# Second attention's query projections: where the modulation sums, the split of the queries and the weight units stand on VectorE and ScalarE

## The reference, cut to what matters

```
sh1, sc1, g1, sh2, sc2, g2 = split(silu(c) @ w_mod[1] + b_mod[1], 6)
h   = modulate(rmsnorm(x, b_norm_g), sh1, sc1)
cq  = rmsnorm(h @ w_dq, q_g)          # 1024 -> 768
q   = (cq @ w_uq)                     # 768  -> 16 heads of 64 + 32
...                                   # rope on the 32, attention, @ w_o
x   = x + g1 * mix
```

## Time and profile before

| | |
|---|---|
| median of 3 runs | 2210.35 us (2209.51 to 2211.14) |
| the profiled execution, its own time | 2212.91 us |
| span of its profile, first to last instruction | 2211.1 us |
| TensorE busy (matmul) | 1876.4 us, 85% of the span |
| VectorE busy | 1505.4 us, 68% |
| ScalarE busy | 848.0 us, 38% |
| GpSimd busy | 561.1 us, 25% |
| mean granted TensorE clock | 0.918 of full speed |
| DMA | 616.18 MB, mean 279 GB/s |
| chain of waits that ended last | TensorE 57%, VectorE 17%, GpSimd 7%, issue 7%, DMA 4%, ScalarE 2% |

### The profile page before, as it was taken

One profiled execution on the slowest core, in us unless ns is written; L12 is line 12 of the kernel. 1 busy time (PEld: TensorE's weight loads), 2 busy tenths in 40 slices (PEclk: granted clock), 3 DMA queues, 4 the chain that ended last, 5 costly groups with the idle time before them and its releaser, 6 DMA issues.

```text
span 2211.1 us, 22537 instructions
## 1 busy us (share of the span) xinstructions
PE 1876.4 (85%) x7847; PEld 1245.6 (56%) x7847; DVE 1505.4 (68%) x2494; ACT 848.0 (38%) x1294; POOL 561.1 (25%) x613
## 2 busy tenths in 40 slices
PE   4998999999978899999996998885786778686786
PEld 1866788888755577888885544682232223232232
DVE  3347778999863775679998995586665565655544
ACT  1354444788634634557783014341221121111120
POOL 0000100000000003030000000036666667666664
PEclk8999999999989999999998999997888888797898
DMA  9761688999855339679994324359999999999997
GB/s 329 273 232 39 239 292 309 392 382 370 321 181 198 127 111 214 206 241 385 379 390 149 118 95 134 124 197 370 360 377 375 377 349 371 360 389 357 369 378 290
DMA packets 193760, 616.18 MB, mean 279 GB/s; under 512 B 19096, under 2 KB 21568, under 8 KB 193008
## 3 DMA queue, kind: packets, MB, share of 16 engines
q1 hardware_dynamic: 114336, 325.98, 40.9%
q0 software_dynamic: 78608, 285.90, 34.8%
q10 hardware_dynamic: 704, 2.86, 0.4%
HBM read 609.43 MB, written 5.25 MB: 278 GB/s over the span
## 4 chain that ended last, share of the span: by engine, by line
PE 57%; DVE 17%; POOL 7%; issue 7%; another core or an unknown queue 6%; DMA 4%; ACT 2%; SPq 0%; DVEq 0%; POOLq 0%; ACTq 0%
PE PS L998 20%; PE PS L1028 10%; DVE peer_rows L2332 6%; PE PS L781 6%; PE PS L802 4%; PE PS L772 4%; POOL peer_rows L713 4%; POOL peer_rows L727 2%; PE PS L1255 2%; DMA peer_rows<-in_peer_u,MOD 1%; DMA ring<-in_w_mod 1%; PE PS L1160 1%; POOL AR L727 1%; PE PS L825 1%
## 5 line engine op out<-in xcount | busy, mean ns | idle before, releaser
L2332 DVE SCALAR_TENSOR_TENSOR peer_rows<-peer_rows,PS 128x1024 f32<-128x1024 f32 x256 | 309.9, 1212 | 80.3 <-DMA peer_rows<-in_peer_u,MOD 73.1
L1974 DVE TENSOR_TENSOR weights_low<-ring,weights_high 128x1024 fp32r<-128x1024 f32 x231 | 280.1, 1229 | 62.2 <-ACT weights_high L1372 59.8
L1372 ACT ACTIVATE weights_high<-ring 128x1024 fp32r<-128x1024 f32 x231 | 242.8, 1061 | 108.8 <-PE PS L998 72.4
L713 POOL DMA_INDIRECT peer_rows<-in_peer_u,MOD x256 | 247.5, 967 | 118.6 <-issue 72.6
L1255 PE MATMUL PS<-peer_rows,HT 128*128 128x512 f32 x368 | 194.5, 663 | 77.0 <-issue 44.1
L1974 DVE TENSOR_TENSOR weights_low_more<-ring,weights_high_more 128x1024 fp32r<-128x1024 f32 x153 | 185.4, 1223 | 36.9 <-ACT weights_high_more L1372 35.4
L1776 DVE TENSOR_TENSOR weights_low<-ring,weights_high 128x1024 fp32r<-128x1024 f32 (+1 forms) x81 | 95.8, 1197 | 139.9 <-ACT weights_high L1279 139.5
L1581 ACT ACTIVATE MOD<-MOD 128x16 f32<-128x16 f32 x16 | 3.4, 215 | 488.7 <-DVE peer_rows L2332 421.6
L1372 ACT ACTIVATE weights_high_more<-ring 128x1024 fp32r<-128x1024 f32 x153 | 161.0, 1060 | 72.8 <-PE PS L998 46.5
L1255 PEld LDWEIGHTS PS<-peer_rows,HT 128*128 128x128 f32 x368 | 74.4, 210 | 193.6 <-issue 184.5
L1255 PE MATMUL PS<-AR,HT 128*128 128x512 f32 x216 | 117.6, 680 | 56.0 <-issue 54.2
(11 more groups left out here) (402 smaller groups left out, 3953.6 us busy)
## 6 DMA issues: line engine op xcount, KB each, us to landing
ring<-in_exp_w_gate SPq DMA_DIRECT2D x128, 512.0 KB, 5.9
ring<-in_exp_w_up SPq DMA_DIRECT2D x128, 512.0 KB, 5.9
ring<-in_exp_w_down SPq DMA_DIRECT2D x128, 512.0 KB, 6.1
ring<-in_w_mod SPq DMA_DIRECT2D x20, 2048.0 KB, 9.1
ring<-in_w_in SPq DMA_DIRECT2D x7, 2048.0 KB, 9.0
ring<-in_a_w_in SPq DMA_DIRECT2D x6, 2048.0 KB, 12.2
ring<-in_kv_w_mod SPq DMA_DIRECT2D x16, 512.0 KB, 5.9
ring<-in_w_mod SPq DMA_DIRECT2D x16, 512.0 KB, 5.3
```

The costliest lines, as they stand in the source:

```text
L713: pool.indirect_dma_start(out=u_row(k), out_offset=None, in_=A["peer_u_2"][0], in_offset=bass.IndirectOffsetOnAxis(ap=EXPERT[:, c, PT_ * h ...
L1372: A_(high_of(n0 + n), raw(ring_slot(layer, m)), ACT.Copy).then_inc(S("moe_high"), 1)
L1974: V.tensor_tensor(low_of(n0 + n), raw(ring_slot(layer, ring_no[layer, "E", n])), high_of(n0 + n).bitcast(fp32), ALU.subtract).then_inc(S(" ...
L2332: V.scalar_tensor_tensor(u_row(k), u_row(k), 1.0, PS[:, 2 * c:2 * c + 2, :].rearrange("p a k -> p (a k)"), ALU.mult, ALU.mult, accum_out=D ...
```

## The change

On ScalarE the high half of the first unit of `b_uq` is written before the copies of `mod1_b`, the high halves of units 1 and 2 behind them as before.

On VectorE four steps move. The wait for the bias and the add of `mod1_a` go from behind the norm of the latent to ahead of the rope on the key. The low halves 3, 4 and 5 of `b_dq` go ahead of the norm of the latent; 6 and 7 stay behind it. The split of the normalised queries goes ahead of the low half of the first unit of `b_uq`. The adds of `mod1_b` go ahead of the low halves 1 and 2.

```diff
@@ ScalarE
         tp("cq")
+        highs("b_uq", 0, 1)
         mod_copies("mod1_b")
-        highs("b_uq", 0, STAGES)
+        highs("b_uq", 1, STAGES)
         evac("b_uq", to_rows(QTOK.rearrange(flat)))
@@ VectorE
         cut_lhs("b_dq", "tp_out", *chunks_out("h_b"))
         lows("b_dq", 1, STAGES)
+        wait("modb1_in", 16 * (MOD_GROUPS + 2))
+        add_mod1("mod1_a")
         wait_evac("kv_down")
...
         last.then_inc(S("key_rope"), 1)
+        lows("b_dq", STAGES, STAGES + 3)
         rms(CKV[:, :, 0:KVR], KVR, CKV[:, :, 0:KVR], "latent", junk=HTm[:, 0:512].rearrange("p (c d) -> p c d", c=C),
             signal="ckv")
-        wait("modb1_in", 16 * (MOD_GROUPS + 2))
-        add_mod1("mod1_a")
-        lows("b_dq", STAGES)
+        lows("b_dq", STAGES + 3)
         wait_evac("b_dq")
         rms(CQ, QR, CQ, "q", junk=HTm[:, 0:2 * QR].rearrange("p (c d) -> p c d", c=C), signal="cq")
+        cut_lhs("b_uq", "tp_out", *chunks_out("cq"))
         lows("b_uq", 0, 1)
-        cut_lhs("b_uq", "tp_out", *chunks_out("cq"))
+        add_mod1("mod1_b")
         lows("b_uq", 1, STAGES)
-        add_mod1("mod1_b")
         lows("b_uq", STAGES)
```

## The result

Four runs of each kernel, taken in turn, gave 2192.32 us for the changed kernel (2189.43 to 2197.24) and 2210.74 us for the one before (2209.51 to 2212.59). The medians lie 18.4 us apart. The ratio is 0.9918, with a 95% interval of 0.9898 to 0.9938, which is between 13.7 and 22.5 us less.

What follows compares the result with a forecast made beforehand. TensorE was taken to bound this stretch, held idle by VectorE's order ahead of two pieces, with half clock behind each. Savings of 4.6 and 8.6 us, together 13.2, off the median 2210.35 gave 2197.1 us; range 2194.8 to 2202.

Steps and rivals of the forecast that it cites:

- First hold: TensorE idle ahead of unit 3 of b_dq, waiting for VectorE's low half; removing it saves 4.6 us, 1.71 of it clock.
- Second hold: TensorE idle ahead of b_uq, waiting for VectorE; starting earlier saves 6.74 us plus 1.83 of clock, 8.6 in sum.
- the clock term: First nine matmuls of b_uq, at half clock after TensorE's idle time, return to full clock: 1.83 us saved.
- The warning against fitting to a number of slow matmuls: Skill's rule that slow-matmul counts vary by run; 3.5 us of clock gain might not count, leaving 9.7 to 13.2.
- the gain's load: GpSimd's load of the queries' gain, released later by the latent's norm; in time even at 14.3 us, so no cost.
- Slab two: Load for b_uq, asked for at about 682; lands before 690.8 even in 8.8 us, in time for unit 3.
- Slab three: Load for b_uq that unit 6 needs by 696.6; expected to land at 692.5, in the times of before.
- one part only: Rival, chance 0.14: half clock stays at b_uq's start (2199 to 2201 us) or a slab is late (2205).
- absorbed: Rival, chance 0.06: a later stage is held by something that has not moved; time 2208 to 2211 us.
- Against: three runs of before lie within 1.6 us: Argument from the spread of the kernel before's total time, set against new half-clock stretches in the second block.
- I let the whole gain through: After b_uq every slab, add and transpose moves with its releasing event, so all 13.2 us reach the total.
- slower: Rival, chance 0.04: arriving earlier, the second block meets 35 us more half clock behind small idle gaps; about 2215 us.

Runs made afterwards that it cites:

- the first hold alone: Kernel before with only the mod1_a add ahead of the rope and b_dq low halves 3 to 5 ahead of the latent's norm; 2206.02 us against 2213.75.
- the filled holds: Kernel before plus 15 unread small products on TensorE ahead of unit 3 of b_dq and 29 ahead of b_uq; ratio 0.9982.
- The other versions: Kernel before with part of the moves or with unread filler products; changed kernel with one move undone or the latent's norm cut in two; ratios 0.9924 to 0.9982.
- the version without the third hold: Changed kernel with the latent's norm cut in two and low half 6 of b_dq between its statistics and scaling; 2128.30 us against 2145.19 of before.

## Why the prediction was wrong, and what of it was right

The terms of the sum came out, 13.2 us of them in every profile. What failed is what was set down for everything outside the stage: the width of the range, and in part the step from the stage to the total. In the changed kernel's first profile everything lies 3.2 us earlier already ahead of the stage, so its times have to be read with that added.

- First hold: forecast 4.6 us. `kv_down` to `b_dq` aside, the stretch up to `kv_up` is 4.4 us shorter (652.07 + 3.2 against 659.66 in the chain), and with the first hold alone the part up to `b_uq` is 4.6 us shorter. The new hold ahead of unit 6 was forecast at 0.9 and is 0.73.
- Second hold: forecast 8.6. `b_uq` starts at 677.92, with 3.2 added at 681.1 (forecast 681.0), with no hold ahead. From there to the attention it is 1.7 us shorter, the clock term that was put at 1.83.
- The clock: full over the stage, and the filled holds show that 3.1 to 3.4 of the 3.5 us were idle time's doing. The warning against fitting to a number of slow matmuls, in the Trainium skill, "TensorE: Matmul & The Clock Gate", section on what is actually happening, made the sum 9.7 to 13.2. In this stage the time did not vary from run to run: the part from `b_uq` to attention takes 40.19 to 40.27 us in five profiles of before. But it came out 0.7 us longer in the kernel with the first hold alone, so the number was not the same for another program.
- The moved wait for the bias, the gain's load (4.1 us after) and the releases of slabs cost nothing, as forecast. Slab two was in time, with low half 3 ready 2.7 us ahead of its need. Slab three took 10.1 us, where the forecast had 8.8, and landed at 686.2, 8 us ahead of TensorE's start on unit 6.
- The rivals "one part only" and "absorbed" did not come.

**The step that failed** is the range. "Against: three runs of before lie within 1.6 us" took three runs for the spread of a measurement, and the lower end, 2.3 us under the forecast, left nothing for the stretches that the change does not touch. In the first measurement these gave 6.6 us in the profile, 3.2 of it ahead of the stage and 3.0 in the gather, which is more than the 2.3. They belong to the executions and not to the change: two profiles of one kernel differ by up to 4.7 us ahead of the stage and 5.4 us in the gather, the 55 runs of before lie between 2204.79 and 2219.93, and the change measured again gave 15.0 and 14.2 us. That the first four runs fell below the range was chance in this sense.

**The step that is in doubt** is "I let the whole gain through", which took the later stages as fixed, 13.2 in and 13.2 out. From attention to gather the changed kernel's profiles are 2.1 us shorter in the mean (0.4 in the first of them), because two of the four lack a half-clock stretch that all five of before have. The other versions come out between 0.3 us longer and 6.4 us shorter than before in the same stretch. So later half-clock time does depend on the execution or on the program, but two against four and none against five do not tell which of the two it is here. The rival "slower" had this mechanism and only its bad side: it priced more half-clock time, and not less. It also put that time behind small idle gaps, and at the one stretch looked at there is none.

Open is why the changed kernel meets that stretch in only two of four profiles, and how much of what the runs show beyond the stage, 1.0 to 1.8 us in the later measurements, is more than chance.

## What to carry to other kernels

When an engine writes operands for several consumers in one hand-made order, put what releases the bottleneck's next instruction first: the add that frees its PSUM banks, then the operand of its next unit, then statistics that are needed later. An idle stretch of the matrix engine has two prices, its own length and half-clock matmuls behind it; here they were about 10 and 3.3 us, and small products whose results nothing reads bought back the second. Judge such a change by the length of its stage in a profile, which repeats to 0.3 us, and give the total a range from many runs, since stages that are not touched may move by as much as the change is worth.

## What the runs showed of the hardware that was not expected

- A stage of 448 us that is bound by TensorE takes 447.9, 444.4 or 442.0 us, according to how much of it runs at half clock (30.7, 23.9 or 17.1 us). With the kernel before it was 447.9 or 448.0 in five of five profiles, with the version without the third hold 442.0 in both of its profiles, and with the first hold alone 442.0 as well. A half-clock stretch in it follows on products that leave TensorE no idle time.
- A hold of 2.74 us on TensorE was followed by 0.54 of the clock and one of 1.61 us was not.
- The kernel before took 2145 us in one group of 13 runs and 2211 to 2214 in the others. The four profiles taken with that group have a gather of 640 us, against 702 to 708; its granted clock was 0.94 to 0.95 and its DMA rate 398 GB/s, against 0.84 and 364 in the first profile of before. The stages ahead of it were the same to within their usual steps. The runs give the same chip number for that group and for the last three executions of before, which took 2211.53 to 2212.55 us a quarter of an hour later, so it does not show that the chip makes the difference. The cause is open.
